# A hybrid decoder step on one core: no closing product per decode lot, two heads' state products side by side, and the elementwise work ahead of the recurrence in 32 pieces

## The chip, the cores and the metric

One core of a Trainium2 chip runs the whole step in one launch. The metric is the device time of that core in microseconds (us). Engines are named as in the profile: PE is TensorE (PEld its weight loads), DVE is VectorE, ACT is ScalarE, POOL is GpSimd, SP is SyncE, which here only issues DMAs.

## The reference

One layer of a hybrid trunk reads 512 prompt tokens (plus 16 learned meta tokens) and 8 running sequences of 8 new tokens each. All arrays are float32, the model width is 1024. Of the normalised input a combined projection makes the inputs of eight forgetting-attention heads and of eight RWKV-7 heads of width 64:

```python
logits = q.k / sqrt(64) + c_q[t] - c_k[s]        # c: running sum of log forget gates
out    = softmax(logits over past pages and own tokens) @ v

kk = k * k_k;  kk = kk / max(norm(kk), 1e-12)    # per head
k  = k * (1 + (a - 1) * k_a)
# per token, state S (64 x 64) of each head
S  = S * decay + (S @ -kk) (kk * a)^T + v k^T;   y = S @ r
out = (groupnorm(y) + sum(r * k * r_k) * v) * g
```

The decode sequences attend to 4096 past tokens each, that is 32 pages of 128 tokens out of a paged cache; keys and values of all pages, 134 MB, pass through the core once. Both head groups go through one output projection, a residual, a SwiGLU feed-forward part of width 2816 and a last norm. The updated RWKV states, the new keys and values and the shift rows are outputs too.

## The kernel before

The step runs in stages. First come the norms, the input projection and the prompt's attention (up to about 329 us in the profiled execution). Then follow, woven together, the decode attention over the cache and all of the RWKV work (329 to 912 us). Last come the output projection and the feed-forward part (912 us to the end), which the change doesn't touch.

**The decode lots.** The sequences are taken in four pairs, each pair's pages in eight lots of four pages: 32 lots. On each engine a lot is a generator of eight pieces. On PE these are: turn the keys of page pair 0 (`turn_keys`, L1178); keys of pair 1 and scores of pair 0 (`page_scores`, L1192); turn the probabilities of the lot before (`turn_probs`, L1218); keys 2 and scores 1; first half of the values of the lot before (`lot_values`, L1237); keys 3 and scores 2; second half of the values; scores 3. After the second half of a lot's values stands one small product, L1241: the identity times a column of ones, added into column 511 of the output bank, which `add_output` doesn't read; its end raises `ov_ready`. In the same pieces ACT copies the turned keys out of PSUM (L1622) and takes the exponentials (L1628), and DVE copies the probabilities (L2131, piece 2), adds a lot's output to the running one (`add_output`, L2141, piece 6) and adds bias to the scores and takes their maximum (`add_scores`, L2100 to L2107, piece 7).

**The rest of the work.** All RWKV work is a second generator per engine (`rwkv_rest`), cut into 140 pieces. After each lot piece every engine takes as many rest pieces as `rwkv_due` says: a straight line, one piece by lot piece 0 and all 140 by lot piece 236 of 256. All engines use the same table, and what they owe each other is kept by semaphores. Each engine works strictly in the order written.

**Ahead of the recurrence.** The first 17 rest pieces are `rwkv_pre`, the elementwise work on 128 x 2560 tiles (four head pairs of 640 token columns): keys scaled and squared, the row sums and their root and reciprocal (L1881, L1502, L1884), eight low-rank products (L868, taken by a sigmoid on ACT, L1495), the norms spread back and multiplied in (L854, L1868), a running sum of the log decays (L1888), three exponentials of 128 x 2560 on ACT (L1517 to L1521), products of all of these (L1893 to L1926, mostly one instruction of 2560 columns each) and the bonus sums (L886, L1872). A tile of the recurrence starts with L962.

**The DMA queue.** SP issues pages in the order in which lots use them, each once the slot it lands in is free. Ahead of a lot's keys stands the load of its forget biases. The bias rows of the second lot land where the low-rank weights lie, so their load, and all that is queued behind it (the keys of the third lot first), waits for the eighth low-rank product to be taken (`lr_taken` at 8).

**The sample states.** Near lot 24 the new states of the 8 running sequences are made, per pair of heads g: DVE spreads two operands per head (`Um`, L2043, two buffers), PE multiplies the keys (L1108) and then the `B` rows (L1109) of head 2g, then those of head 2g+1, each 64 rows by 64 columns by 512, and DVE adds and scales (L2031, L2035).

## Time and profile before

| what | value |
|---|---|
| median of 3 runs | 1510.46 us (1509.58 to 1511.0) |
| profiled execution | 1510.73 us, of which the span from first to last instruction is 1509.0 us |
| mean granted TensorE clock | 0.969 |
| PE busy | 1402.4 us, 93% of the span |
| DVE, ACT, POOL busy | 438.2 us, 357.0 us, 110.0 us |
| DMA | 219.32 MB, 145 GB/s over the span |

The busy share is a mean over stages with different limits. From 984 us to the end PE runs almost without a gap; the stretch in which the other engines and the DMA queues matter lies between 329 and 912 us, and that is where the changed lines are.

### The profile page before, as it was taken

To read this page: it belongs to the slowest core of one execution; us is meant where nothing else is said; L and a number is where in the kernel's file an instruction comes from. 1 tells how busy PE (TensorE), PEld (TensorE's weight loads), DVE (VectorE), ACT (ScalarE), POOL (GpSimd) and SP (SyncE) were. 2 spreads that over 40 slices of the span, in tenths; PEclk is the share of its full clock that TensorE was granted. 3 is DMA by queue.
4 is the path that set the end of the run, shared out by engine and by line. 5 is a ranking of instruction groups with operands and counts; after the bars stand their busy time and mean duration, and the time that the engine had idled before them with its cause. 6 is when DMAs were issued, how large, how long until landed. Compare 5 with 4: busy or idle time off the path is not lost.

```text
span 1509.0 us, 27895 instructions
## 1 busy us (share of the span) xinstructions
PE 1402.4 (93%) x11595; PEld 953.3 (63%) x11595; DVE 438.2 (29%) x917; ACT 357.0 (24%) x713; POOL 110.0 (7%) x223
## 2 busy tenths in 40 slices
PE   5999999988799999999989779999999999999997
PEld 4755666655577777777755454477777777744442
DVE  5022355455844444444445241310000000000002
ACT  3010233245444343443433331100000000000011
POOL 6283000000000000001202010000000000000000
PEclk9999899998799999999989889999999999999998
DMA  5187011023898787878957897003111221150001
GB/s 206 57 189 205 7 57 35 1 75 110 284 312 277 229 292 247 294 255 266 272 191 261 315 314 245 1 13 100 56 56 56 89 79 56 56 195 0 0 0 63
DMA packets 123174, 219.32 MB, mean 145 GB/s; under 512 B 11451, under 2 KB 35078, under 8 KB 123046
## 3 DMA queue, kind: packets, MB, share of 16 engines
q1 hardware_dynamic: 115154, 193.64, 38.3%
q0 software_dynamic: 7824, 23.85, 5.9%
q8 instruction: 92, 1.51, 0.4%
q14 instruction: 36, 0.29, 0.1%
q10 hardware_dynamic: 68, 0.02, 0.0%
HBM read 203.06 MB, written 14.41 MB: 144 GB/s over the span
## 4 chain that ended last, share of the span: by engine, by line
PE 84%; DVE 5%; DMA 4%; ACT 3%; issue 2%; SPq 1%; POOL 0%; DVEq 0%; POOLq 0%; ACTq 0%
PE PS L1369 23%; PE PS L736 13%; PE PS L1388 10%; PE PS L1178 6%; PE PS L1192 4%; PE PS L1308 4%; PE PS L1237 4%; PE PS L709 2%; DMA arena<-in_cache_k 2%; DMA out_wkv_prompt<-arena 1%; PE PS L1394 1%; PE PS L992 1%; PE PS L1002 1%; PE PS L996 1%; ACT arena L1622 1%
## 5 line engine op out<-in xcount | busy, mean ns | idle before, releaser
L1369 PE MATMUL PS<-arena 128*128 128x288 f32 x1408 | 342.1, 405 | 1.2 <-DVE arena L2251 1.2
L1369 PEld LDWEIGHTS PS<-arena 128*128 128x128 f32 x1408 | 265.7, 189 | 77.4 <-DVE arena L2251 1.4
L736 PE MATMUL PS<-arena 128*128 128x301 f32 (+1 forms) x736 | 197.7, 426 | 0.0
L1622 ACT ACTIVATE arena<-PS 128x512 f32<-128x512 f32 x256 | 141.4, 596 | 192.8 <-PE PS L1178 192.4
L1178 PE MATMUL PS<-arena 128*128 128x128 f32 x1024 | 153.8, 296 | 27.1 <-DMA arena<-in_cache_k 15.1
L736 PEld LDWEIGHTS PS<-arena 128*128 128x128 f32 (+1 forms) x736 | 136.6, 189 | 54.7 <-issue 13.6
L1178 PEld LDWEIGHTS PS<-arena 128*128 128x128 f32 x1024 | 122.1, 151 | 55.8 <-issue 24.2
L1388 PE MATMUL PS<-arena 128*128 128x512 f32 x352 | 151.5, 592 | 1.5 <-DVE arena L2277 1.5
L1388 PEld LDWEIGHTS PS<-arena 128*128 128x128 f32 x352 | 66.5, 189 | 86.2 <-issue 84.3
L2277 DVE TENSOR_TENSOR arena<-PS,arena 128x576 f32<-128x576 f32 x22 | 16.7, 758 | 327.0 <-ACT arena L1686 327.0
L1686 ACT ACTIVATE arena<-PS 128x576 f32<-128x576 f32 x22 | 14.3, 651 | 329.8 <-PE PS L1369 329.8
L1192 PE MATMUL PS<-arena 128*32 128x128 f32 x2048 | 85.7, 286 | 3.8 <-ACT arena L1622 2.4
L1237 PE MATMUL PS<-arena 128*32 128x256 f32 x1024 | 69.7, 389 | 2.8 <-DMA arena<-in_cache_v 2.8
L1192 PEld LDWEIGHTS PS<-arena 128*32 128x32 f32 x2048 | 50.0, 112 | 24.8 <-issue 19.3
L1308 PE MATMUL PS<-arena 128*128 128x512 f32 x128 | 55.8, 593 | 0.0
L1952 DVE TENSOR_TENSOR arena<-PS,arena 128x512 f32<-128x512 f32 (+2 forms) x56 | 35.9, 659 | 41.3 <-PE PS L992 20.6
L2297 DVE TENSOR_TENSOR arena<-PS,arena 128x512 f32<-128x512 f32 x8 | 5.5, 692 | 143.2 <-PE PS L1388 143.2
L363 POOL DMA_DIRECT2D out_y_prompt<-arena x4 | 2.1, 537 | 596.0 <-DVE arena L2286 596.0
L1671 ACT ACTIVATE arena<-arena 128x1024 f32<-128x1024 f32 x8 | 8.4, 1045 | 151.4 <-DVE arena L2297 137.7
L1237 PEld LDWEIGHTS PS<-arena 128*32 128x32 f32 x1024 | 29.5, 111 | 22.3 <-issue 6.4
L1308 PEld LDWEIGHTS PS<-arena 128*128 128x128 f32 x128 | 23.9, 189 | 29.1 <-issue 29.1
L1434 ACT ACTIVATE arena<-PS 128x602 f32<-128x602 f32 (+1 forms) x23 | 15.5, 673 | 108.3 <-PE PS L736 108.3
(360 smaller groups left out, 1409.9 us busy)
## 6 DMA issues: line engine op xcount, KB each, us to landing
arena<-in_cache_k SPq DMA_DIRECT2D x256, 256.0 KB, 4.3
arena<-in_cache_v SPq DMA_DIRECT2D x256, 256.0 KB, 4.8
arena<-in_w_gate SPq DMA_DIRECT2D x11, 1024.0 KB
arena<-in_w_up SPq DMA_DIRECT2D x11, 1024.0 KB
arena<-in_w_in SPq DMA_DIRECT2D x5, 2048.0 KB, 11.9
forgets_after<-arena POOLq DMA_DIRECT2D x64, 128.0 KB, 8.5
arena<-forgets_after SPq DMA_DIRECT2D x32, 256.0 KB, 5.1
arena<-in_w_down SPq DMA_DIRECT2D x4, 2048.0 KB
```

Of the source, the lines that this page charges most:

```text
L709: ins = mm(o, xnT[:, k, 17 + P * (i - 1):17 + P * i], w, start=(k == 0), stop=(k == KT - 1))
L736: ins = mm(PS[0:width, bank, 0:HALF], wring[:, c % 2, k, c0:c0 + width], xnT[:, k, half * HALF:(half + 1) * HALF], start=(k == 0), stop=(k ...
L1178: ins = tr(PS[:, bank, g * P:(g + 1) * P], Kr[:, i, q, g * P:(g + 1) * P], ident)
L1192: ins = mm(PS[ROWS[2 * q + gp], SCORE, i * P:(i + 1) * P], QB[:, 2 * (L // NLOT) + q, g, :], KTs[:, (2 * i + q) % LOT, g, :], start=(gg == ...
L1237: ins = mm(PS[ROWS[r], OUT, 0:QW], PTs[:, i, ROWS[r]], Vr[:, i, r // 2, QW * (r % 2):QW * (r % 2) + QW], start=(i == 0), stop=(i == LOT - ...
L1308: ins = mm(PS[rows, E + 2 * (n % 2) + half, :], mixT[:, k, cols], wo[:, k, half * NB:(half + 1) * NB], start=(k == 0), stop=(k == KT - 1))
L1369: ins = mm(PS[:, 4 * (f % 2) + 2 * w + half, 0:HO], fring[r % FR][:, c:c + P], hT[:, k, half * HO:(half + 1) * HO], start=(k == 0), stop=( ...
L1388: ins = mm(PS[:, 4 * half + n, :], actT[:, k, cols], w_down(half, k), start=(k == 0), stop=(k == NF - 1))
L1434: av(dst.rearrange("p (a b) -> p a b", a=2), src, ACT.Copy, scale=scale).then_inc(S["proj_taken"], 1)
L1622: av(KTs[:, (2 * i + q) % LOT], PS[:, T_USE[("k", L, i, q)] % 2, :].rearrange("p (g n) -> p g n", g=NG), ACT.Copy)\
L1952: return tt(dst, src, mask.unsqueeze(1).unsqueeze(1).to_broadcast([n_p, a, b, n]), ALU.mult)
L2277: tt(actT[:, f, :].rearrange("p (a b) -> p a b", a=2), PS[:, 4 * (f % 2) + 2:4 * (f % 2) + 4, 0:HO], sgate[:, f % 2, :].rearrange("p (a b) ...
```

## The change

Three edits. (1) The product L1241 is gone; `add_output` now waits for `v_free`, the semaphore that the last value product of the lot raises anyway. (2) The sample state products of head 2g and 2g+1 are issued alternately, keys of both, then `B` rows of both, after one wait for both heads' operands. (3) `rwkv_pre` has 32 pieces in place of 17. Its operations of 2560 columns are cut into two of 1280 (the reciprocal into two of 320), the running sums stand one to a piece, and empty pieces on PE and ACT keep step with DVE. `rwkv_due` gives two rest pieces to lot piece 0 and one to each of the next 30; the other 123 pieces follow on a straight line, complete by lot piece 235. The order of SP's and POOL's instructions is the same as before.

```diff
-        N_PRE = 17
+        N_PRE = 32
...
         def rwkv_due(piece):
-            return min(N_RWKV, 1 + piece * (N_RWKV - 1) // (8 * LOTS - 20))
+            if piece < N_PRE - 1:
+                return piece + 2
+            left, pieces = N_RWKV - N_PRE - 1, 8 * LOTS - 20 - N_PRE
+            return min(N_RWKV, N_PRE + 1 + (piece - N_PRE + 1) * left // pieces)
...
-                if half:
-                    mm(PS[:, OUT, 511:512], ident, ones[:, 0:1], start=False, stop=True, skip_group_check=True).then_inc(S["ov_ready"], 1)
...
             def add_output(L):
                 q = L // NLOT % 2
-                dve.wait_ge(S["ov_ready"], L + L // NLOT + 2)
+                dve.wait_ge(S["v_free"], LOT * (L + 2))
...
                 for g in range(NG):
-                    for hp in range(2):
-                        h = 2 * g + hp
-                        hc = slice(h * HD, (h + 1) * HD)
-                        pe.wait_ge(S["um_ready"], h + 1)
...
+                    pe.wait_ge(S["um_ready"], 2 * g + 2)
+                    if g >= 2:
+                        pe.wait_ge(S["sn_taken"], g - 1)
+                    for w, u in ((K_, 1), (B_, 0)):
+                        for hp in range(2):
+                            hc = slice((2 * g + hp) * HD, (2 * g + hp + 1) * HD)
+                            ins = mm(PS[64 * hp:64 * hp + 64, E + 2 + g % 2, :], nat_[64:P, w, hc],
+                                     Um[64:P, hp, u].rearrange("p b i -> p (b i)"), start=(u == 1), stop=(u == 0), skip_group_check=True)
...
-                v.reciprocal(Rn, Rn).then_inc(S["hs_in"], 1)
+                ch(v.reciprocal(Rn[:, 0:HT], Rn[:, 0:HT]))
+                yield
+                v.reciprocal(Rn[:, HT:TL], Rn[:, HT:TL]).then_inc(S["hs_in"], 1)
+                yield
+                norm_keys(0)
+                yield
+                for g in range(3):
+                    dve.wait_ge(S["lr_taken"], g + 1)
+                    ch(v.tensor_tensor_scan(Kd[:, g], chunk_mask, AR[:, 0, g], 0.0, ALU.mult, ALU.add))
+                    norm_keys(g + 1)
+                    yield
...
-                ch(tt(Bd, Bd, kk, ALU.mult))
+                for p in pair:
+                    ch(tt(Bd[:, p], Bd[:, p], kk[:, p], ALU.mult))
+                    yield
```

On PE, around the second lot: keys (L1178, after the change L1186), scores (L1192, then L1200), probabilities (L1218, then L1226), values (L1237, then L1245), low-rank products (L868, then L871) and spread norms (L854, then L857). Before:

```order
L1218 MATMUL PS<-arena 128x128 x4
L1178 MATMUL PS<-arena 128x128 x8
L1192 MATMUL PS<-arena 32x128 x8
L868 MATMUL PS<-arena 128x320 x2
L854 MATMUL PS<-arena 128x320 x2
L1237 MATMUL PS<-arena 32x256 x8
L868 MATMUL PS<-arena 128x320 x2
L1178 MATMUL PS<-arena 128x128 x8
L1192 MATMUL PS<-arena 32x128 x8
L1237 MATMUL PS<-arena 32x256 x8
L1241 MATMUL PS<-arena 128x1
L1192 MATMUL PS<-arena 32x128 x8
```

The same place after the change, from the lot's second key pages on:

```order
L1186 MATMUL PS<-arena 128x128 x8
L1200 MATMUL PS<-arena 32x128 x8
L871 MATMUL PS<-arena 128x320 x2
L1226 MATMUL PS<-arena 128x128 x4
L1186 MATMUL PS<-arena 128x128 x8
L1200 MATMUL PS<-arena 32x128 x8
L1245 MATMUL PS<-arena 32x256 x8
L1186 MATMUL PS<-arena 128x128 x8
L1200 MATMUL PS<-arena 32x128 x8
L1245 MATMUL PS<-arena 32x256 x8
L1200 MATMUL PS<-arena 32x128 x8
```

The last low-rank product stood behind the first half of the values, in lot piece 12; it now stands ahead of the lot's probabilities, in lot piece 9. The closing product ahead of the last scores is gone.

On DVE, the pieces behind the low-rank products, in lots 1 and 2: L1902 and L1905 to L1915 are elementwise work, L2141 is `add_output`, L2100 to L2107 `add_scores`, L2125 and L2127 the running sums, L2131 the copy of the probabilities. Before:

```order
L1902 TENSOR_SCALAR arena<-arena 128x640 x4
L2141 SCALAR_TENSOR_TENSOR arena<-arena,PS 128x256
L1905 SCALAR_TENSOR_TENSOR arena<-arena 128x2560
L2100 TENSOR_TENSOR arena<-PS,arena 128x512
L2103 TENSOR_REDUCE arena<-arena 128x1
L2107 TENSOR_SCALAR arena<-arena 128x1
L1909 SCALAR_TENSOR_TENSOR arena<-arena 128x640 x4
L2125 SCALAR_TENSOR_TENSOR arena<-arena 128x1
L2127 TENSOR_TENSOR arena<-arena 128x1
L1913 TENSOR_TENSOR arena<-arena 128x2560
L2131 COPY arena<-PS 128x512
L1915 SCALAR_TENSOR_TENSOR arena<-arena 128x2560
```

After the change the same lines are L1916, L2169, L1921, L2128 to L2135, L1926, L2153 and L2155, L2159 and L1934:

```order
L1916 TENSOR_SCALAR arena<-arena 128x640 x4
L2169 SCALAR_TENSOR_TENSOR arena<-arena,PS 128x256
L1921 SCALAR_TENSOR_TENSOR arena<-arena 128x1280
L2128 TENSOR_TENSOR arena<-PS,arena 128x512
L2131 TENSOR_REDUCE arena<-arena 128x1
L2135 TENSOR_SCALAR arena<-arena 128x1
L1921 SCALAR_TENSOR_TENSOR arena<-arena 128x1280
L1926 SCALAR_TENSOR_TENSOR arena<-arena 128x640 x2
L2153 SCALAR_TENSOR_TENSOR arena<-arena 128x1
L2155 TENSOR_TENSOR arena<-arena 128x1
L1926 SCALAR_TENSOR_TENSOR arena<-arena 128x640 x2
L2159 COPY arena<-PS 128x512
```

Between two operations of a lot there now stand one or two halves where one or two whole operations stood.

On PE, the sample state products of the third pair of heads (L1108 and L1109 before, L1115 after). Before:

```order
L1178 MATMUL PS<-arena 128x128 x16
L1192 MATMUL PS<-arena 32x128 x8
L1108 MATMUL PS<-arena 64x512
L1109 MATMUL PS<-arena 64x512
L1108 MATMUL PS<-arena 64x512
L1109 MATMUL PS<-arena 64x512
L1218 MATMUL PS<-arena 128x128 x4
```

After the change:

```order
L1186 MATMUL PS<-arena 128x128 x8
L1115 MATMUL PS<-arena 64x512 x4
L1186 MATMUL PS<-arena 128x128 x8
L1200 MATMUL PS<-arena 32x128 x8
L1226 MATMUL PS<-arena 128x128 x4
```

This group of four moved one lot piece up, ahead of the second key pages; the first two groups keep their lot piece.

## Rows read from the trace of the kernel before

**Rows 1.** Stretch, us; busy PE, PEld, DVE, ACT, POOL; PE clock, DMA share, GB/s.

```profile
335.61:415.62 80.01, 65.74 (x555) 43.42 (x555) 53.69 (x58) 41.03 (x56) 1.75 (x5) 0.80 0.60 206
421.00:774.00 353.00, 332.66 (x6383) 260.28 (x6381) 148.48 (x321) 149.38 (x295) 13.36 (x17) 1.00 0.82 269
```

**Rows 2.** PE's waits in 802 to 912 us: total, times, longest.

```profile
PE PS L1178 <- DMA arena<-in_cache_k: 7.9, 3, 5.3
PE PS L1237 <- DMA arena<-in_cache_v: 2.8, 3, 1.3
```

**Rows 3.** The closing product by line: busy, mean ns, idle before.

```profile
L1241 PE MATMUL PS<-arena 128*128 128x1 f32 x64 | 12.3, 261 | 0.0
```

**Rows 4.** PE in time, end of lot 2: start, us, count.

```profile
395.26 1.09 PE L1178 MATMUL PS<-arena 128*128 128x128 f32 x8
396.28 0.65 PE L1192 MATMUL PS<-arena 128*32 128x128 f32 x16
396.75 1.05 PE L1237 MATMUL PS<-arena 128*32 128x256 f32 x16
397.72 0.38 PE L1241 MATMUL PS<-arena 128*128 128x1 f32 x2
398.04 0.65 PE L1192 MATMUL PS<-arena 128*32 128x128 f32 x16
398.61 1.09 PE L1178 MATMUL PS<-arena 128*128 128x128 f32 x8
```

**Rows 5.** Busy time by stretch: lots 0, 1, 2 and 3 up to L962.

```profile
335.61:360.27 24.66, 21.16 (x150) 12.80 (x151) 15.82 (x13) 12.68 (x17) 0.00 (x0) 0.78 0.64 220
360.27:382.28 22.01, 17.54 (x155) 11.36 (x154) 12.49 (x15) 15.60 (x18) 0.00 (x0) 0.89 0.21 66
382.28:398.61 16.33, 13.81 (x134) 9.73 (x134) 13.31 (x16) 7.73 (x12) 0.00 (x0) 0.61 1.01 359
398.61:415.62 17.01, 13.23 (x121) 9.53 (x117) 12.07 (x16) 5.03 (x10) 1.75 (x5) 0.90 0.63 220
```

**Rows 6.** PE in time, waits in brackets, elementwise stretch.

```profile
350.99 1.34 PE L854 MATMUL PS<-arena 32*128 32x320 f32 x4 [0.67 <-DVE arena L1884]
...
357.88 2.46 PE L854 MATMUL PS<-arena 32*128 32x320 f32 x4 [2.64 <-DVE arena L1868]
...
382.28 3.83 PE L1178 MATMUL PS<-arena 128*128 128x128 f32 x16 [3.98 <-DMA arena<-in_cache_k]
...
407.68 3.57 PE L886 MATMUL PS<-arena 128*128 128x320 f32 x8 [3.78 <-DVE arena L1872]
```

**Rows 7.** ACT and SP in time: last low-rank sigmoid, bias load.

```profile
374.98 0.80 ACT L1495 ACTIVATE arena<-PS,arena 128x640 f32<-128x640 f32 x1 [2.76 <-PE PS L868]
...
375.80 0.82 SPq L428 DMA_DIRECT2D arena<-forgets_after  x2
```

**Rows 8.** DVE by line and shape, 335.61 to 415.62 us.

```profile
L1888 DVE TENSOR_TENSOR_SCAN arena<-arena 128x640 f32<-128x640 f32 x4 | 5.6, 1472 | 0.3 <-ACT arena L1495 0.3
L1909 DVE SCALAR_TENSOR_TENSOR arena<-arena 128x640 f32<-128x640 f32 x4 | 3.3, 878 | 0.0
L1905 DVE SCALAR_TENSOR_TENSOR arena<-arena 128x2560 f32<-128x2560 f32 x1 | 2.8, 2818 | 0.0
```

**Rows 9.** Sample states in time, second and third pair of heads.

```profile
782.40 2.32 PE L1108 MATMUL PS<-arena 64*64 64x512 f32 x3 [2.79 <-DVE arena L2043]
...
787.21 3.83 PE L1178 MATMUL PS<-arena 128*128 128x128 f32 x16
...
790.93 2.50 DVE L2043 TENSOR_TENSOR arena<-arena 64x512 f32<-64x512 f32 x4
...
792.28 1.07 PE L1108 MATMUL PS<-arena 64*64 64x512 f32 x2 [0.65 <-DVE arena L2043]
...
793.49 0.64 PE L1108 MATMUL PS<-arena 64*64 64x512 f32 x1
...
795.35 0.66 PE L1218 MATMUL PS<-arena 128*128 128x128 f32 x4
```

More of the change, by code:

```diff
@@ L889, in rwkv_pre @@
             def rwkv_pre():
-                yield
+                for _ in range(3):
+                    yield
                 row_sums_of(T2, 1, E + 2)
@@ L905, in rwkv_pre @@
                 yield
-                for _ in range(6):
+                for _ in range(8):
                     yield
@@ L910, in rwkv_pre @@
                 yield
+                for _ in range(9):
+                    yield
                 bonus_sums(2)
                 bonus_sums(3)
+                yield
                 yield
@@ L1497, in rwkv_pre @@
             def rwkv_pre():
-                yield
+                for _ in range(3):
+                    yield
                 low_rank(0)
@@ L1505, in rwkv_pre @@
                 yield
-                low_rank(3)
                 yield
-                low_rank(4)
+                for j in range(3, 8):
+                    low_rank(j)
+                    yield
                 yield
-                low_rank(5)
-                yield
-                low_rank(6)
-                yield
-                low_rank(7)
                 yield
@@ L1522, in rwkv_pre @@
                 yield
-                for _ in range(7):
+                for _ in range(16):
                     yield
@@ L1900, in rwkv_pre @@
                 dve.wait_ge(S["lr_taken"], 8)
-                for g in range(NG):
-                    ch(ts(T2[:, g], Bd[:, g], -1.0, pc("k_a", g), ALU.add, ALU.mult))
-                yield
-                ch.wait()
-                ch(stt(XR[:, 4:8], T2, 1.0, XR[:, 4:8], ALU.add, ALU.mult))
-                yield
-                ch.wait()
-                for g in range(NG):
-                    ins = stt(T2[:, g], XR[:, g], pc("r_k", g), XR[:, 4 + g], ALU.mult, ALU.mult)
-                ins.then_inc(S["hs_in"], 1)
@@ L1921, in rwkv_pre @@
-                ch(tt(Bd, Bd, Kd, ALU.mult))
-                yield
-                ch(tt(AR[:, 1], XR[:, 0:4], AR[:, 1], ALU.mult))
-                yield
-                ch.wait()
-                ch(tt(Kd, XR[:, 4:8], Kd, ALU.mult))
-                yield
+                for p in pair:
+                    for g in range(p.start, p.stop):
+                        ch(ts(T2[:, g], Bd[:, g], -1.0, pc("k_a", g), ALU.add, ALU.mult))
+                    yield
+                for p in pair:
+                    ch.wait()
+                    w = slice(4 + p.start, 4 + p.stop)
+                    ch(stt(XR[:, w], T2[:, p], 1.0, XR[:, w], ALU.add, ALU.mult))
+                    yield
@@ new lines, in rwkv_pre @@
+                for p in pair:
+                    ch.wait()
+                    for g in range(p.start, p.stop):
+                        ins = stt(T2[:, g], XR[:, g], pc("r_k", g), XR[:, 4 + g], ALU.mult, ALU.mult)
+                        if g < 3:
+                            ch(ins)
+                    if p.stop == NG:
+                        ins.then_inc(S["hs_in"], 1)
+                    yield
+                dve.wait_ge(S["decays"], 3)
+                for p in pair:
+                    ch(tt(Bd[:, p], Bd[:, p], kk[:, p], ALU.mult))
+                    yield
@@ new lines, in rwkv_pre @@
+                for p in pair:
+                    ch(stt(AR[:, 0, p], kk[:, p], -1.0, AR[:, 0, p], ALU.mult, ALU.mult))
+                    if p.start == 0:
+                        ch(v.tensor_copy(Dc[:, :, 0:1], AR[:, 1, :, NMETA - 1:NMETA]))
+                        ch(v.tensor_copy(Dc[:, :, 1:1 + DB], AR[:, 1, :, 64 + DS - 1:P:DS]))
+                        ch(v.tensor_copy(Dc[:, :, 1 + DB:], AR[:, 1, :, P + 63:TL:64]))
+                    yield
+                for p in pair:
+                    ch.wait()
+                    ch(tt(Bd[:, p], Bd[:, p], Kd[:, p], ALU.mult))
+                    yield
@@ L1928, in rwkv_pre @@
+                for p in pair:
+                    ch.wait()
+                    ch(tt(AR[:, 1, p], XR[:, p], AR[:, 1, p], ALU.mult))
+                    yield
+                for p in pair:
+                    ch.wait()
+                    ch(tt(Kd[:, p], XR[:, 4 + p.start:4 + p.stop], Kd[:, p], ALU.mult))
+                    yield
                 add_bonus(0)
@@ L1932, in rwkv_pre @@
                 add_bonus(3)
+                yield
                 ch.wait()
```

41 lines of the change are left out of this document (17 added, 24 removed).

## Prediction, made before the changed kernel was timed

> **What bounds the kernel now.** I read busy time by stretch first, since a share over the whole span mixes stages. Two stretches differ. In 421 to 774 us, most of the woven decode and recurrence part, PE is busy 332.66 of 353 us at full clock [rows 1]: PE is the bound, and an instruction taken off PE there comes off the time. In 335.61 to 415.62 us, the lots that share the engines with the elementwise work, PE is busy 65.74 of 80.01 us and its granted clock is only 0.80 [rows 1]: PE waits, and pays twice, since it comes back from long waits at the lower of its two clock levels, 1.2 GHz (a spread product takes 2.46 us behind a wait of 2.64 us and 1.34 us behind one of 0.67 us [rows 6]). So I then read who is waited for there: a running sum on DVE (2.64 us), keys by DMA (3.98 us) and the bonus products on DVE (3.78 us) [rows 6]. Last, from 802 to 912 us, PE's waits for page DMAs alone come to 10.7 us [rows 2]: what PE saves ahead of such a wait is waited for instead.
>
> **The closing product.** L1241 has 64 records, two per product, so 32 products of 0.38 us busy each, with no idle time before them [rows 3]. What one is worth is the step from its start to the next instruction's: 398.04 - 397.72 = 0.32 us [rows 4]. `add_output` loses nothing: its new semaphore is raised by the product just before. Of the 32, two lie in the elementwise stretch and are counted there. Four (those in lots 26, 27, 29 and 30) stand ahead of the waits for DMA after 802 us, which end at their own time [rows 2]; I give them nothing. The other 26 give 26 x 0.32 = 8.3 us. Between none hidden (30 x 0.32 = 9.6) and all given back as waits (0) I take 8.3, because PE has hardly any idle time in the stretch where 20 of them lie.
>
> One more effect could be in this edit. Scores take 0.47 us when values of the same 128 x 32 shape follow (396.28 to 396.75), but 0.57 us when a 128 x 128 product follows (398.04 to 398.61) [rows 4]. The Trainium skill, TensorEngine Tiling (Array Packing), Key Properties, says why that may be: changing the tiling mode drains the engine. By that rule the sixteen lots in which scores followed directly on L1241 would gain about 0.1 us more each, 1.6 us in all, and the sum would be 1493.7 us. The two rows agree with it, but none shows values followed by scores, so I leave it out of the sum.
>
> **The elementwise stretch.** It runs through lots 0 to 3. I walk through it on the rows' durations at full clock: keys of one page pair 1.02 us, scores 0.57, values 0.97 [rows 4], probabilities half of the keys, 0.51, a low-rank or spread product about 1.3 [rows 6]. A lot's own PE work without the closing product is then 4 x 1.02 + 4 x 0.57 + 2 x 0.97 + 0.51 = 8.8 us. On DVE the four running sums take 5.6 us and stand in one piece; an operation on 2560 columns takes 2.8 us [rows 8]. Cutting costs something: four instructions of 640 columns are busy 3.3 us where one of 2560 takes 2.8, so 0.15 us more for each extra instruction; nine cuts, 1.4 us.
>
> Lot 0, 24.66 us before [rows 5]. Up to the first spread at 350.99 us nothing moves, because row sums, root and reciprocal are one chain that PE already waits for [rows 6]. Behind it PE waited 2.64 us for all four running sums and came back at half clock. Now one sum of 1.4 us stands ahead of each norm, and PE has its low-rank and spread products to do meanwhile: from 352.3 us, 4 x 1.3 us, scores 0.6 and the new tokens' values 0.6 end at 358.8. So 23.2 us, with two more low-rank products done.
>
> Lot 1, 22.01 us before. Its end was the wait of 3.98 us for keys. They came late because SP's bias load waits for the eighth low-rank sigmoid, which ended at 375.78, and went out at 375.80 [rows 7]; meanwhile the DMA engines were busy 0.21 of the time, and in the next lot 1.01 [rows 5]. The eighth product moves from lot piece 12 to piece 9; by my walk its sigmoid ends near 368 us, the keys can be in use 6.5 us later, as they were before (375.80 to 382.28) [rows 6, 7], so near 374, when PE comes to them. PE's own work is 8.8 + three products of 1.3 = 12.7 us; ACT, with three exponentials on 2560 columns, is the later one, and was busy 15.6 us in this lot before [rows 5]. The walk gives 15.3 us.
>
> Lot 2, 16.33 us before. DVE sets it: it was busy 13.31 us [rows 5] and is given one half more (1.5 us) and four cuts, 15.4 us, and PE waits for the last exponential on ACT. The walk gives 16.1 us: no gain here beyond the closing product.
>
> Lot 3, 17.01 us before up to the first recurrence tile. That tile now comes two lot pieces later, behind values (1.0) and scores (0.6), so 18.6 us is what to compare with. DVE has four halves, the bonus products and the memsets behind each other; the walk gives 18.9 us. The wait of 3.78 us goes, but the second pair of bonus sums, now in the piece just ahead of DVE's second pair of additions, waits for DVE's queue instead.
>
> Together 23.2 + 15.3 + 16.1 + 18.9 = 73.5 us against 80.0 + 1.6 = 81.6: a gain of 8.1 us. The walk is at full clock; waits of 1 to 3 us stay, after which some products run at 1.2 GHz; I take 1 us off for that and enter 7.1 us. Bounds: nothing (81.6), and DVE never waiting in lots 1 to 3, where it was busy 12.49 + 13.31 + 12.07 us and gets 1.4 on top: 39.3 us, with lot 0 62.5, a gain of 19.1. Behind the stretch the recurrence starts two pieces later and ends one piece earlier, at nearly the same density; I enter nothing.
>
> **The sample states.** DVE makes the operands of a pair of heads in 2.50 us; PE starts the first head when its half is there (792.28) and the second at 793.49, and the next work follows at 795.35 [rows 9]. So the second head's own passes take 1.86 us, and the first head's run beside them already. With both heads started at 793.49 the group ends at 795.35 too: zero. The bounds are a loss of 1.21 us per group if the alternating products get in each other's way (4.8 us for four), and a gain if DVE were ahead.
>
> The Trainium skill would have that gain: TensorEngine Tiling (Array Packing), Key Properties, says that different tiles execute independently, weight loads and products in parallel. The trace agrees that they overlap, and for that reason already in the old order; the page names no wait for operands.
>
> **Sum.** 8.3 + 7.1 + 0 = 15.4 us. The profiled execution took 1510.73 us (span 1509.0 and 1.7 around it), 0.27 above the median of the runs; 1510.7 - 15.4 = 1495.3 us. The likeliest case's own range is 1489 to 1501.
>
> **Rivals.**
> - Only the closing products count (1501.7). DVE has the same work plus 1.4 us, so its queue moves PE's waits from one piece to the next and the stretch stays as long; 28 x 0.32 = 9.0 us come off (all but the four). For it: DVE was busy 53.69 of 80.01 us [rows 1] and sets lots 2 and 3 in my walk. Against: the 3.98 us for keys hang on one early release, not on DVE. Chance 0.17.
> - The stretch gives all that DVE allows: 19.1 + 8.3 off, 1483.3 us. For it: pieces of 1.5 us fit into PE's 8.8 us per lot everywhere. Against: ACT's three long exponentials are not cut. Chance 0.11.
> - The sample operands are ready early, and side by side pays: each group then costs 1.86 us and not 3.07 (792.28 to 795.35), the group at 1.2 GHz twice 1.86 and not 4.81 [rows 9]; 3 x 1.21 + 1.09 = 4.7 us more, 1490.6 us. Against: PE waits for DVE at both starts in the rows. Chance 0.07. This is the way it would go by the Trainium skill's rule on independent tiles.
> - No change (1510): a lot's period is the loop scores, maximum, exponential, probabilities, and what PE saves comes back as waits in it, in the stretch too. Against: PE idles 20 us in 353 [rows 1]. Chance 0.05.
> - Slower: in lots 1 to 3 DVE now always holds a half, so PE gets many short waits, and its clock stays at 1.2 GHz through them. PE's work there in my walk, some 35 us, takes 70 us where the walk has 50.3: 20 us more, 1515 us. It decides from the point where three quarters of those lots run at 1.2 GHz. For it: lot 2 had a clock of 0.61 before [rows 5]. Against: that low clock stood behind the wait for keys. Chance 0.05.
>
> **How the numbers follow.** The forecast has 0.55. What a measurement of this kernel can tell from no change is about 0.2%, 3 us, so faster means below 1507.4: the forecast and the first three rivals, 0.90, less 0.02 for their tails. Same gets 0.05 + 0.02, slower 0.05. The range leaves out half of the second rival and both last ones: 1484 to 1507 us.
>
> **What would show it.** The chain and the lines must have no L1241, and the step from values to scores must be gone. In the stretch up to the first L970 (the old L962), the bias load behind the last low-rank sigmoid must go out some 8 us earlier, and the first key product of lot 2 must not wait for DMA; the stretch itself should be near 73.5 us long with a clock above 0.80. In the sample states, PE should wait about 1.2 us longer at each start and end each group as before. 421 to 774 us should shrink by about 0.32 us per lot and PE's idle time there stay near 20 us. I am wrong if that idle time grows by what the closing products were worth, or if DVE's work shows PE's waits in lots 2 and 3 to be longer than the ones that went.

## The result and the profile after

The changed kernel took 1523.54 us, median of 4 runs (1518.33 to 1530.8), against 1510.47 (1509.58 to 1511.0) for the kernel before: a ratio of 1.009, 95% interval 1.0046 to 1.0135. It is slower by 7 to 20 us, where 15 us faster was forecast, and its single runs lie 12 us apart. On a second chip the two stood at 1520.91 and 1510.04 us, a ratio of 1.0059 (1.0034 to 1.0084). One execution of 2046.56 us, among the twelve of the kernel with an early bias load and the recurrence two pieces ahead further down, lies far outside the rest and is left out of that kernel's ratio.

The profiled execution took 1518.33 us (span 1516.5). Its mean granted clock of TensorE was 0.957, where the kernel before had 0.969.

To compare stretches I cut them at two events that both kernels have: PE's first row-sum product, and the addition of lot 3's scores on DVE. Of before, and then of after (columns as in [rows 1]):

```profile
340.24:419.69 79.45, 65.19 (x588) 42.48 (x580) 53.73 (x61) 39.76 (x54) 1.75 (x5) 0.83 0.59 201
```

```profile
339.25:420.25 81.00, 70.06 (x558) 43.67 (x549) 52.80 (x66) 38.97 (x52) 0.14 (x1) 0.75 0.60 205
355.00:360.00 5.00, 5.00 (x30) 1.96 (x28) 3.75 (x6) 0.00 (x0) 0.00 (x0) 0.50 0.08 31
360.00:365.00 5.00, 5.00 (x14) 3.10 (x14) 2.50 (x3) 1.66 (x3) 0.00 (x0) 0.50 0.00 0
365.00:370.00 5.00, 5.00 (x11) 2.47 (x11) 0.47 (x2) 3.14 (x5) 0.00 (x0) 0.50 0.00 0
370.00:375.00 5.00, 5.00 (x28) 2.99 (x27) 2.05 (x4) 2.64 (x5) 0.00 (x0) 0.50 0.02 3
375.00:380.00 5.00, 5.00 (x44) 3.49 (x44) 3.99 (x5) 3.42 (x5) 0.00 (x0) 0.50 0.53 161
```

PE's idle time in the stretch fell from 14.3 to 10.9 us, as intended, and PE had 30 records less. Yet its busy time grew by 4.9 us. From 355 to 380 us PE is busy in every microsecond and has 1.2 GHz throughout. PE in order of time, after (start, us, form, count):

```profile
352.07 1.43 PE L871 MATMUL PS<-arena 64*128 64x320 f32 x4
353.44 2.49 PE L857 MATMUL PS<-arena 32*128 32x320 f32 x4
355.86 1.08 PE L1200 MATMUL PS<-arena 128*32 128x128 f32 x16
356.87 1.08 PE L1234 MATMUL PS<-arena 64*32 64x256 f32 x8
357.88 2.50 PE L871 MATMUL PS<-arena 64*128 64x320 f32 x4
360.31 2.50 PE L857 MATMUL PS<-arena 32*128 32x320 f32 x4
362.73 1.97 PE L1186 MATMUL PS<-arena 128*128 128x128 f32 x8
```

L871 are the low-rank products (64 rows of the array), L857 the spread products (32 rows). A spread product took 1.34 us at full clock [rows 6], and a low-rank product as much; here either takes 2.5. No wait stands between them, and the last one before them ended at 348.36 us: the clock fell at about 353 us in the middle of work. The last low-rank sigmoid therefore ended as late as before [rows 7], and the bias load went out at 375.75 us, not 8 us earlier:

```profile
374.93 0.79 ACT L1501 ACTIVATE arena<-PS,arena 128x640 f32<-128x640 f32 x1 [1.54 <-PE PS L871]
...
375.75 0.81 SPq L431 DMA_DIRECT2D arena<-forgets_after  x2
```

The prediction measured the stretch from the first key product of lot 0 to the first recurrence tile, and had it near 73.5 us. Here it takes 85.57 us:

```profile
334.62 3.84 PE L1186 MATMUL PS<-arena 128*128 128x128 f32 x16 [2.67 <-DMA arena<-in_cache_k]
...
420.19 1.09 PE L970 MATMUL PS<-arena 64*64 64x128 f32 x16 [1.33 <-DVE arena L1964]
```

The first key products of lots 1, 2 and 3 start at 362.73, 383.73 and 400.54 us. So lots 0 to 3 take 28.1, 21.0, 16.8 and 19.7 us, where the walk had 23.2, 15.3, 16.1 and 18.9: nearly all of the excess lies in lots 0 and 1, where the clock was low.

In 421 to 774 us PE's idle time is 21.7 us, near the 20.3 of before [rows 1]:

```profile
421.00:774.00 353.00, 331.33 (x6376) 259.06 (x6374) 150.59 (x324) 151.14 (x297) 14.19 (x21) 1.00 0.81 269
```

The four groups of the sample states now wait 1.30, 3.99, 0.69 and 3.32 us for DVE, where only two of them waited before (2.79 and 0.65 us), and three of the four then run wholly or partly at 1.2 GHz (3.68, 3.67 and 3.20 us for a group, 1.94 at full clock). The first two, to be compared with [rows 9]:

```profile
773.47 1.94 PE L1115 MATMUL PS<-arena 64*64 64x512 f32 x8 [1.30 <-DVE arena L2071]
...
782.59 3.68 PE L1115 MATMUL PS<-arena 64*64 64x512 f32 x8 [3.99 <-DVE arena L2071]
```

### The profile page after: what moved, and what is told of

It is laid out like the page before. It is cut to its first block, busy times and chain, and to the rows that moved or that the text cites. A ratio compares the mean times of both kernels' runs of the same rounds, so it can differ in the third digit from the quotient of the medians.

```text
span 1516.5 us, 27778 instructions
## 1 busy us (share of the span) xinstructions
PE 1405.3 (93%) x11531; PEld 951.7 (63%) x11531; DVE 438.7 (29%) x926; ACT 358.4 (24%) x713; POOL 110.1 (7%) x223
## 4 chain that ended last, share of the span: by engine, by line
PE 85%; DVE 5%; ACT 3%; DMA 3%; issue 2%; SPq 1%; POOL 0%; DVEq 0%; POOLq 0%; ACTq 0%
PE PS L1375 23%; PE PS L739 12%; PE PS L1394 10%; PE PS L1186 7%; PE PS L1200 4%; PE PS L1314 4%; PE PS L1245 4%; PE PS L712 2%; PE PS L1400 1%; DMA arena<-in_cache_k 1%; DMA arena<-in_cache_v 1%; PE PS L1010 1%; PE PS L1000 1%; PE PS L1004 1%; ACT arena L1626 1%
## 5 line engine op out<-in xcount | busy, mean ns | idle before, releaser
L1186 PE MATMUL PS<-arena 128*128 128x128 f32 x1024 | 154.2, 295 | 35.7 <-DVE arena L2159 13.5
L739 PEld LDWEIGHTS PS<-arena 128*128 128x128 f32 (+1 forms) x736 | 135.7, 188 | 54.2 <-issue 12.7
L1186 PEld LDWEIGHTS PS<-arena 128*128 128x128 f32 x1024 | 121.6, 150 | 67.0 <-issue 32.6
L1690 ACT ACTIVATE arena<-PS 128x576 f32<-128x576 f32 x22 | 14.3, 652 | 332.7 <-PE PS L1375 332.7
L1200 PE MATMUL PS<-arena 128*32 128x128 f32 x2048 | 87.9, 291 | 1.6 <-DVE arena L2146 0.8
L1245 PE MATMUL PS<-arena 128*32 128x256 f32 x1024 | 72.1, 399 | 4.4 <-DMA arena<-in_cache_v 4.4
L1200 PEld LDWEIGHTS PS<-arena 128*32 128x32 f32 x2048 | 52.8, 114 | 26.9 <-issue 19.6
L1245 PEld LDWEIGHTS PS<-arena 128*32 128x32 f32 x1024 | 30.0, 113 | 24.6 <-issue 7.7
```

The costliest lines, as they stand in the source:

```text
L739: ins = mm(PS[0:width, bank, 0:HALF], wring[:, c % 2, k, c0:c0 + width], xnT[:, k, half * HALF:(half + 1) * HALF], start=(k == 0), stop=(k ...
L1186: ins = tr(PS[:, bank, g * P:(g + 1) * P], Kr[:, i, q, g * P:(g + 1) * P], ident)
L1200: ins = mm(PS[ROWS[2 * q + gp], SCORE, i * P:(i + 1) * P], QB[:, 2 * (L // NLOT) + q, g, :], KTs[:, (2 * i + q) % LOT, g, :], start=(gg == ...
L1245: ins = mm(PS[ROWS[r], OUT, 0:QW], PTs[:, i, ROWS[r]], Vr[:, i, r // 2, QW * (r % 2):QW * (r % 2) + QW], start=(i == 0), stop=(i == LOT - ...
```

## Experiments

Ratios are to the kernel before, run on the same chip, with 95% intervals; differences in us are the ratio less one, times the median of before there (1510 to 1512 us).

### Each edit by itself

**The first edit alone.** The kernel before with the two lines of the closing product taken out and DVE's two waits set to match:

```diff
-                if half:
-                    mm(PS[:, OUT, 511:512], ident, ones[:, 0:1], ...).then_inc(S["ov_ready"], 1)
...
-                dve.wait_ge(S["ov_ready"], L + L // NLOT + 2)
+                dve.wait_ge(S["v_free"], LOT * (L + 2))
...
-                dve.wait_ge(S["ov_ready"], (NLOT + 1) * pr + 1)
+                dve.wait_ge(S["ov_ready"], pr + 1)
```

> The kernel before with the first edit alone: the 32 closing products are gone. Theory A (each closing product was worth its step of 0.32 us wherever PE has no idle time): 8 to 9 us come off, 1501 to 1503 us, and PE's idle time in the woven part stays near 20 us. Rival B (PE is not the bound of a lot: what it saves comes back as waits): 1509 to 1512 us. Rival C (the loss of the whole change lies in this edit, because the full-array product helped to hold the clock up): 1515 us or more, with a lower granted clock in lots 4 to 23.

Measured: 1505.54 us, 0.9957 (0.9935 to 0.9979), so 6.5 us less (3.2 to 9.8): theory A in its mechanism, its 8 to 9 us at the upper end. Lots 4 to 8 by the windows of before and of this kernel (both from one addition of scores on DVE to another):

```profile
419.69:498.88 79.19, 74.99 (x1422) 58.27 (x1425) 34.39 (x72) 34.01 (x69) 0.00 (x0) 1.00 0.85 287
```

```profile
419.52:497.04 77.52, 73.31 (x1412) 56.87 (x1414) 34.34 (x73) 33.99 (x69) 0.00 (x0) 1.00 0.87 295
```

Five lots, five closing products, 1.67 us: 0.33 us each. Its granted clock there is 1.00, as it is on to lot 23, so rival C falls. In these two profiles the gain is larger than the run's: from the first row-sum product to the scores of lot 31 the kernel before takes 571.91 us and this one 563.91, 8.0 us less; behind that point, where both do the same work, this one takes 2.8 us more (599.68 against 596.85), most of it at the first gate and up products (last section).

**The second edit alone.**

```diff
-                    for hp in range(2):
...
-                        pe.wait_ge(S["um_ready"], h + 1)
...
+                    pe.wait_ge(S["um_ready"], 2 * g + 2)
...
+                    for w, u in ((K_, 1), (B_, 0)):
+                        for hp in range(2):
...
```

> The kernel before with the second edit alone: each pair of sample heads waits for both operands and runs side by side. Theory A (the trace of the changed kernel shows four waits on DVE there, a granted clock of 0.50 from 780 to 806 us, and lot 25 6.0 us longer): 3 to 6 us slower, 1513.5 to 1516.5 us. Rival B (the group ends when it did, as predicted; what is longer in lot 25 came from rest work left over from earlier): 1509.5 to 1511.5 us. Rival C (side by side pays): below 1508 us.

Measured: 1513.72 us, 1.0003 (0.9982 to 1.0024): 0.5 us more, between 2.7 less and 3.6 more. That is nothing that can be measured. It fits rival B, and theory A is out but for its lower end.

**The third edit alone.** The changed kernel with the closing products and the old order of the sample heads put back.

> The kernel before with the third edit alone: the elementwise work in 32 pieces, closing products and the old order of the sample states kept. Theory A (the loss lies in the elementwise stretch: PE stays at 1.2 GHz for about 27 us there, though it is busy): 8 to 15 us slower, 1518 to 1525 us, with granted clock 0.50 from about 355 to 380 us and single runs some us apart. Rival B (the stretch gains its 7 us and the loss is elsewhere): 1503 to 1506 us. Rival C (the closing product between values and scores holds the clock up in the stretch, so that with it the pieces do no harm): 1508 to 1511 us and a clock above 0.75 from 355 to 380 us.

Measured: 1525.28 us, 1.0081 (1.0051 to 1.0112): 12.3 us more (7.7 to 16.9). Theory A; the clock is 0.50 in each 5 us from 355 to 380 us, with PE busy 5.00 of 5, closing products or not. The loss lies in this edit.

**The first two edits without the third.**

> The changed kernel without its third edit: no closing products and the sample heads side by side, elementwise work in 17 pieces as before. Theory A (the three edits add up: closings -8, heads +3 to +6): 1505 to 1508 us. Rival B (all of the loss is the pieces): 1501 to 1503 us. Rival C (the pieces do no harm): 1520 us or more, as the changed kernel.

Measured: 1510.17 us, 0.9986 (0.9962 to 1.0009): 2.1 us less, between 5.7 less and 1.4 more: rivals B and C are out, and theory A's sum fits, though the loss that it gives the heads did not show in the run of the second edit alone. The three edits by themselves add up to -6.5 + 0.5 + 12.3 = +6.3 us; all of them together are 8.9 (5.1 to 12.7) on the second chip.

### Why PE is slow in the pieces

**Full rows.** Same products, same columns, same result, but over all 128 rows, with weights that GpSimd pads with zeros beforehand:

```diff
+            ch(g.memset(WZ, 0.0))
+            ch(g.memset(SZ, 0.0))
+            for r in range(2):
+                ch(g.tensor_copy(WZ[64 * r:64 * r + 64, r], WA[64 * r:64 * r + 64]))
+            for q in range(NG):
+                ch(g.tensor_copy(SZ[32 * q:32 * q + 32, q], spread[32 * q:32 * q + 32]))
...
-                    ins = mm(..., spread[rows], Rn[rows, ...
+                    ins = mm(..., SZ[:, g], Rn[:, ...
...
+                if j == 0:
+                    pe.wait_ge(S["pool_c"], WIDE[0])
...
-                    ins = mm(..., WA[rows, w], XR[rows, 12, ...
+                    ins = mm(..., WZ[:, j // 4, w], XR[:, 12, ...
```

> The changed kernel, but its 8 low-rank and 4 spread products of the elementwise stretch contract over all 128 rows instead of 64 and 32: GpSimd copies their weights into blocks padded with zeros beforehand, so each product has the same columns, the same result and the same number of passes. Theory A (PE stays at 1.2 GHz there because most of its work uses few of the array's rows): granted clock above 0.85 from 355 to 380 us, these products near 1.3 us and not 2.5, and the kernel 8 to 14 us below the changed one, 1509 to 1516 us. Rival B (the clock follows the many small pieces and waits, whatever the rows): clock 0.50 as before, 1522 to 1525 us.

Measured: 1508.87 us, 0.9983 (0.9965 to 1.0002); the changed kernel beside it had 1520.91. 12.0 us less by the medians, by no other edit than the rows and the padding ahead of them (the new wait for GpSimd's copies shows no idle time on PE). The windows, and PE in order of time (L883 low-rank, L868 spread):

```profile
343.73:412.47 68.74, 55.10 (x558) 36.77 (x549) 52.58 (x67) 38.15 (x52) 0.07 (x1) 0.91 0.71 241
355.00:360.00 5.00, 5.00 (x36) 2.95 (x38) 3.40 (x4) 1.59 (x2) 0.00 (x0) 1.00 0.79 285
360.00:365.00 5.00, 5.00 (x30) 3.51 (x23) 4.93 (x8) 2.06 (x4) 0.00 (x0) 1.00 0.09 33
```

```profile
354.57 1.35 PE L883 MATMUL PS<-arena 128*128 128x320 f32 x4
355.75 1.24 PE L868 MATMUL PS<-arena 128*128 128x320 f32 x4
```

The stretch takes 68.74 us, with 558 records; in the two profiles of the changed kernel it takes 81.00 us (558 records) and 77.89 us (559, the one on the same chip). Theory A holds, and rival B is out.

**Filler.** The narrow products as they are, and a product of 128 rows ahead of each but the first:

```diff
+            def fill(bank):
+                mm(PS[:, bank, 0:256], ident, XR[:, 8, 0:256], start=True, stop=True, ...)
```

> The changed kernel with 11 more products in the elementwise stretch, of 128 rows, 128 columns of weights and 256 columns, one ahead of each low-rank (but the first) and each spread product, into the bank that this product then overwrites: at full clock about 0.5 us each, 5.6 us of work that nothing needs. Theory A (rows of the array hold the clock): the clock from 355 to 380 us rises above 0.75 and the kernel comes out no slower than the changed one, 1513 to 1523 us, in spite of the added work. Rival B (the rows don't matter): clock 0.50, the fillers take 1 us each, 8 to 12 us slower than the changed kernel.

Measured: 1514.63 us, 1.0028 (1.0006 to 1.005): 6.3 us below the changed kernel by the medians, though PE has 11 products more (L861 here). The intervals of the two ratios overlap, so the size of that gain is uncertain; the clock is not, it is 1.00 in each 5 us from 355 to 380 us:

```profile
342.84:416.46 73.62, 61.62 (x582) 38.76 (x574) 52.88 (x66) 39.01 (x53) 0.14 (x1) 0.95 0.68 229
360.00:365.00 5.00, 5.00 (x38) 2.51 (x37) 3.99 (x6) 0.79 (x1) 0.00 (x0) 1.00 0.01 2
```

```profile
361.73 0.70 PE L861 MATMUL PS<-arena 128*128 128x256 f32 x2
362.36 1.34 PE L876 MATMUL PS<-arena 64*128 64x320 f32 x4
...
364.26 1.34 PE L857 MATMUL PS<-arena 32*128 32x320 f32 x4
```

So narrow products run at full clock when full-row work stands between them: it is the long run of them that PE does at 1.2 GHz, not the single product.

**The old order with full rows.** The first edit and full rows in the order of before.

> The kernel before without its closing products (the first edit alone) and with the low-rank and spread products over all 128 rows. Theory A: in the order of before these products ran at full clock but for one behind the wait of 2.64 us, so little is to be had: 0 to 3 us below the first edit alone, 1499 to 1505 us. Rival B (a wait brings the clock down and the rows of what follows don't matter): the same as the first edit alone, 1502 to 1507 us.

Measured: 1502.21 us, 0.9933 (0.9908 to 0.9959). The intervals of this and of the first edit alone (0.9957) overlap; the times fit either expectation.

**The changed kernel again**, beside these three.

> The changed kernel as it is, on the same chip as the three others, so that they can be set against it and not only against the kernel before. By all theories 1518 to 1526 us, 8 to 16 us above the kernel before, with granted clock 0.50 from about 355 to 380 us.

Measured: 1520.91 us, 1.0059 (1.0034 to 1.0084), with a clock of 0.50 from 355 to 370 us.

### Where the forecast gain of the stretch is

**An early bias load in the old order.** The padded copies make the original low-rank weights, which lie where the second bias lands, free early:

```diff
                 elif j == 1:
-                    sp.wait_ge(S["lr_taken"], 8)
+                    sp.wait_ge(S["pool_c"], 97)
```

> The kernel before without closing products, low-rank and spread products over 128 rows, and SyncE's second bias load waits only for GpSimd's copies of the low-rank weights (it lands where the original weights lie), not for the eighth sigmoid. The 17 pieces and their order stay. If the 3.98 us that PE waited for keys hang on this one release, as the prediction has it, the wait of 4.5 us ahead of lot 2's keys goes without any cutting of the elementwise work: 2 to 5 us below the same kernel with the late release, 1497 to 1501 us where that had 1502. Rival (the wait is only passed on, to ACT's exponentials, as the changed kernel shows 3.36 us behind them): no change, 1501 to 1504 us, with a wait of 3 us or more on ACT in its place.

Measured: 1502.07 us, 0.9931 (0.9907 to 0.9956), the same as without it. The load went out at 354.85 us, and PE waited nonetheless. The wait ahead of lot 2's keys, first with the late load and then with the early one:

```profile
379.24 3.38 PE L1190 MATMUL PS<-arena 128*128 128x128 f32 x16 [4.49 <-DMA arena<-in_cache_k]
```

```profile
385.41 1.94 PE L1190 MATMUL PS<-arena 128*128 128x128 f32 x8 [4.53 <-ACT arena L1632]
```

This is the rival's case: L1632 is ACT's copy of turned keys, which stands behind the long exponentials. In the changed kernel the same wait has 3.36 us.

**Pieces, full rows, old order of the heads** (the changed kernel with full rows less its second edit).

> The first and the third edit with the low-rank and spread products over 128 rows, sample heads in the old order: the changed kernel with full rows less its second edit. If the second edit costs 2 to 4 us in this setting: 1505 to 1507 us. If it costs nothing: 1508 to 1510 us, as with it.

Measured: 1507.37 us, 0.9973 (0.9956 to 0.9989): the expectation for a second edit that costs something, but the interval overlaps that of the run with it (0.9983). Its windows show what the stretch is worth: to lot 3, to lot 12, lots 13 to 17, and lots 18 to 31. First the old order with full rows, then the pieces:

```profile
339.18:417.44 78.26, 61.47 (x584) 41.52 (x576) 53.62 (x62) 39.84 (x54) 1.74 (x5) 0.87 0.58 203
339.18:562.03 222.85, 197.61 (x3331) 147.81 (x3322) 116.30 (x193) 102.81 (x179) 1.74 (x5) 0.95 0.75 256
562.03:649.50 87.47, 83.16 (x1600) 66.05 (x1604) 39.10 (x88) 34.43 (x69) 0.00 (x0) 0.98 0.76 257
649.50:901.68 252.18, 216.90 (x3113) 154.28 (x3112) 103.51 (x204) 100.30 (x185) 24.78 (x35) 0.94 0.81 275
```

```profile
339.49:410.02 70.53, 57.22 (x560) 38.71 (x549) 52.66 (x66) 38.38 (x52) 0.07 (x1) 0.88 0.69 235
339.49:553.10 213.61, 193.21 (x3243) 144.90 (x3232) 117.01 (x202) 100.94 (x176) 1.74 (x5) 0.96 0.78 264
553.10:648.42 95.32, 87.58 (x1694) 68.72 (x1691) 39.05 (x88) 36.29 (x71) 0.00 (x0) 0.96 0.75 246
648.42:906.16 257.74, 221.95 (x3112) 155.26 (x3111) 103.53 (x204) 100.54 (x185) 24.74 (x35) 0.91 0.80 268
```

Each kernel has one profile here, and they are from two chips. The pieces lead by 7.7 us at lot 3 and 9.2 at lot 12, but PE has then done 88 records less (3243 against 3331). In lots 13 to 17 it does them (1694 against 1600), with 7.7 us of idle time against 4.3, 2.9 of them one wait of a recurrence step for DVE. At lot 17, with 4937 records against 4931, the lead is 310.32 - 308.93 = 1.4 us; against the old order with the early bias load, which gets there in 306.25 us with 4936 records, it is a lag of 2.7 us. Behind it the same work takes 5.6 us longer, nearly all of it clock (0.91 against 0.94; idle 35.8 and 35.3). Most of that last part varies between profiles, and the old order with the early bias load took 257.75 us for it too. One piece of it is steady: lots 24 to 26 take 73.50 us at a clock of 0.84 here, and 71.93 us at 0.91 in the old order. In the five profiles with neither the pieces nor the heads side by side these lots take 71.85 to 72.40 us at 0.90 to 0.93; in the eight with one or both (and the recurrence not moved ahead) 73.50 to 76.19 us at 0.80 to 0.88. Why the clock is lower there, these runs don't show.

With full rows the clock can fall too. In this run it was 0.50 from 350 to 353 us, after a wait of 1.66 us that ended at 348.44 us; it was back at 1.00 by 354 us while PE worked on. With the narrow rows it stayed at 0.50 for 25 us.

**The recurrence two pieces ahead**, with the early bias load.

```diff
+            ahead = 0 if piece < N_PRE + 8 else 1 if piece < N_PRE + 16 else 2
-            return min(N_RWKV, N_PRE + 1 + (piece - N_PRE + 1) * left // pieces)
+            return min(N_RWKV, N_PRE + 1 + ahead + (piece - N_PRE + 1) * left // pieces)
```

> As the run with the recurrence two pieces ahead, and with the early bias load as well. In the 32 pieces the keys of lot 2 no longer waited for DMA, but PE waited for ACT there; so the early load gives nothing more: within 2 us of the run without it. If it does give something, 2 to 4 us less.

Measured: 1515.98 us, 1.0029 (1.0012 to 1.0046); with the table alone 1514.94, 1.0028 (1.001 to 1.0047).

> The first and third edit with full rows, sample heads in the old order (1507 us, 0.9973 of before), and from lot piece 40 on the recurrence one and from 48 on two pieces ahead of the changed kernel's table, so that it is no longer behind the old one. Theory (the late recurrence costs a wait of 2.9 us where a pair of lots changes, and what was put off is paid for in lots 12 to 17): 2 to 5 us off, 1502 to 1505 us. Rival (put-off work costs the same wherever it is done): 1506 to 1509 us. With the early bias load as well it took 1516 us: if that lies in the table, 1513 to 1518 us here.

A table that is two pieces ahead from the end of the 32 pieces on deadlocks (engines wait for each other in a circle), so it has no time.

So the load costs and gives nothing, and the table costs 8 us (0.9973 without it). The theory's gain is not there: the wait of 2.9 us stays (waits of PE: us in total, times, longest), and the table brings a new wait of PE behind the recurrence. ACT, which works in the order written, now comes early to the square of 128 x 2560 that has to wait until the prompt's new states are written out (12.12 us, 6.94 us without the table), and the copies of turned keys that PE needs in lot 27 stand behind it (L1199 are key turns):

```profile
PE PS L1023 <- DVE arena L1993: 3.1, 2, 2.9
```

```profile
831.76 2.34 ACT L1621 ACTIVATE arena<-arena 128x2560 f32<-128x2560 f32 x1 [12.12 <-DMA out_wkv_prompt<-arena]
```

```profile
835.32 1.94 PE L1199 MATMUL PS<-arena 128*128 128x128 f32 x8 [10.91 <-ACT arena L1639]
```

**Filled waits in the old order.** Products that nothing needs, put into three of PE's long waits, on top of the first edit and full rows:

```diff
+                if (L, i) == (2, 0):
+                    pe.wait_ge(S["ov_taken"], 2)
+                    fill(OUT, XR[:, 8, 0:256], 7)
                 pe.wait_ge(k_in[i], 32 * (L + 1))
...
+                pe.wait_ge(S["ov_taken"], 3)
+                fill(OUT, XR[:, 8, 0:256], 6)
                 bonus_sums(2)
...
+            fill(E + 3, mixT[:, 0, 0:256], 2)
             turn_h(4)
+            fill(E + 3, mixT[:, 0, 0:256], 2)
```

> The order of before without closing products and with 128-row low-rank and spread products (1502 us, 0.9933 of before), and with products that nothing needs put into PE's own long waits: 7 ahead of the keys of lot 2, 6 ahead of the third bonus product, 2 and 2 around the last turn ahead of gate and up, each of 128 rows, 128 columns of weights and 256 columns (about 0.5 us). Theory (PE comes back from a long wait at 1.2 GHz, and filling the wait keeps it at full clock for free): granted clock from 380 to 390 us above 0.9 (0.66 and 0.68 without), the third and fourth bonus products 2.3 us and not 4.6, clock 1.00 at the first gate and up products, and 2 to 6 us off: 1496 to 1500 us. Rival (what runs at 1.2 GHz there lies beside DVE's and ACT's work, which sets the end): the rows get faster but the time stays within 1501 to 1503 us.

Measured: 1498.13 us (1494.2 to 1504.96), 0.9925 (0.9894 to 0.9955). The third and fourth bonus products without and with it:

```profile
404.52 4.61 PE L898 MATMUL PS<-arena 128*128 128x320 f32 x8 [3.78 <-DVE arena L1882]
```

```profile
401.32 2.76 PE L1189 MATMUL PS<-arena 128*128 128x256 f32 x12
405.28 2.40 PE L898 MATMUL PS<-arena 128*128 128x320 f32 x8 [1.20 <-DVE arena L1893]
```

The rows do what was expected there, and the clock at the first gate and up products is 1.00; but from 385 to 390 us it is 0.77, behind waits for ACT that I had not filled. The median is in the expected range; against 0.9933 without the fillers the gain isn't shown. It has the lowest median here, some 11 us below the kernel before on the same chip (7 to 16).

## Why the prediction was wrong

**The step that failed** is the one of the elementwise stretch: "The walk is at full clock; waits of 1 to 3 us stay, after which some products run at 1.2 GHz; I take 1 us off for that". I knew one way to the low clock, a wait, and priced that. The change took PE's waits away and put the twelve narrow products close together, and PE fell to 1.2 GHz in the middle of them and stayed there.

The sign stood in the trace of the kernel before, and I read it wrongly. I put the spread product of 2.46 us [rows 6] down to the wait of 2.64 us ahead of it. But the low-rank product ahead of that wait already took 1.82 us, so the clock had fallen before the wait began; in the old order with full rows the same product in the same place took 1.35 us. First before, then with full rows:

```profile
353.41 1.82 PE L868 MATMUL PS<-arena 64*128 64x320 f32 x4
```

```profile
352.23 1.35 PE L880 MATMUL PS<-arena 128*128 128x320 f32 x4
```

A wait brings the clock down as well: behind it (3.11 us there) the spread product took 2.47 us with full rows too, at a granted clock of 0.50. By line, busy in the stretch, after (32 and 16 records each):

```profile
L871 PE MATMUL PS<-arena 64*128 64x320 f32 x32 | 14.0, 576 | 0.0
L857 PE MATMUL PS<-arena 32*128 32x320 f32 x16 | 8.8, 695 | 0.0
```

and with full rows:

```profile
L883 PE MATMUL PS<-arena 128*128 128x320 f32 x32 | 10.4, 451 | 0.0
...
L868 PE MATMUL PS<-arena 128*128 128x320 f32 x16 | 5.0, 434 | 0.0
```

That is 22.8 against 15.4 us, 7.4 of the 12.3 us by which the stretches of these two profiles differ; keys, scores and values between them, and what waits for them, make the rest.

**The walk itself** was right, once the narrow products no longer hold the clock down. With full rows lots 0 to 3 take 23.6, 14.4, 15.9 and 19.4 us, 73.3 in all (75.1 in the run with the old order of the heads), where the walk had 73.5. In the latter run the bias load goes out at 367.56 us, where I had it near 368. This is shown by changing the rows alone.

**A second step failed with it**: "Behind the stretch the recurrence starts two pieces later and ends one piece earlier, at nearly the same density; I enter nothing". The late start had to be entered as work put off. At equal work, in lot 17, the pieces with full rows are 1.4 us ahead of one profile of the old order and 2.7 us behind the other. So even with full rows this term was worth about nothing there and not 7.1 us, and the whole kernel is slower for the pieces (below). By the medians the narrow rows account for 12.0 of the miss of some 24 us on the second chip (15.4 us less forecast, 8.9 us more measured), and the pieces with full rows for about as much (7.1 us forecast as a gain, 5.3 us measured as a loss).

**The keys' wait.** I argued that the 3.98 us "hang on one early release, not on DVE". The release was not enough: ACT's copies behind its exponentials end 4.5 us late as well, and the early load showed it. I had ACT as the later engine in lot 1 of the walk, and "ACT's three long exponentials" against a rival, but left ACT out of this argument.

**The closing products** were sized right: 8.3 us forecast, 6.5 (3.2 to 9.8) measured, and 8.0 up to lot 31 in the profiles. What I had not seen is the 2.8 us behind that point. The side effect that I left out of the sum is there. The step from values to the following scores is 0.86 us in this kernel of the first edit (903.42 - 902.56), where values took 0.97 [rows 4]:

```profile
902.56 1.05 PE L1237 MATMUL PS<-arena 128*32 128x256 f32 x16
903.42 0.62 PE L1192 MATMUL PS<-arena 128*32 128x128 f32 x16
```

The Trainium skill, TensorEngine Tiling (Array Packing), Key Properties, has it that a change of tiling mode drains the engine; values and scores here have the same tile shape, and the row agrees, by 0.1 us. In the time it can't be seen.

**The sample states** came out as forecast, at nothing (0.5 us, -2.7 to 3.6), and the waits grew by 1.2 us as said (2.79 to 3.99). What I had not said is that PE then runs the group at 1.2 GHz more often; in the profile of the second edit alone lots 24 to 26 take 73.64 us and before 72.40, but the timing can't tell 1 us from nothing.

**The slower rival** (1515 us, chance 0.05) had the right place and sign: PE at 1.2 GHz through most of lot 1. Its reason, many short waits, was wrong, since PE had none from 353 to 380 us, and so it got too small a chance.

**What stays open.** With full rows the pieces are at 0.9973 (0.9956 to 0.9989), and the old order with the same products at 0.9933 (0.9908 to 0.9959). On the chip of the pieces the old order with the early load is at 0.9931 (0.9907 to 0.9956). So the forecast gain of 7 us is not there even with full rows: by the medians on that chip the pieces are 5.3 us slower, and the intervals meet only at their ends. The profiles put the difference behind lot 17, into the clock. Some 1.6 us of it, in lots 24 to 26, is steady; the rest varies between profiles of one kernel by more than that (258.94 and 266.81 us behind lot 17 in the two of the changed kernel), so where it arises stays open.

## What to carry to other kernels

Before packing small products closer together, look at how many rows of the array each uses: here a run of 64- and 32-row products cost PE half its clock though it never idled, and zero-padded weights of full rows, or full-row products in between, gave it back. A low clock behind a wait need not come from the wait: look at the last product ahead of it first. A lead inside a woven stretch counts only at equal work, so compare two orders at a point where both have done the same number of instructions. Where a wait ends with one engine, find out who would end it next before giving it a price.

## What the runs showed of the hardware

- PE was busy 5.00 of 5 us in five successive stretches and had 1.2 GHz in all of them; twelve products over 128 rows instead of 64 and 32 brought 2.4 GHz, and so did 11 useless full-row products between the narrow ones, with which the kernel was 6.3 us faster by the medians (the intervals overlap).
- Ahead of the first gate and up products PE does the same instructions with the same two waits (1.41 and 1.20 us) in every kernel but the one that fills them. Its clock in the 10 us around them was 1.00 in the profiles of the three kernels with closing products, and 0.66 or 0.83 in nine of the eleven profiles without them and without fillers there. After the change ACT had the first of their results 18.8 us after the first of these products (988.88 to 1007.68), before it 15.8 us (984.25 to 1000.09). I did not find the cause; with four full-row products in the two waits the clock was 1.00.
- The kernel before ranges from 1504.69 to 1521.49 us over 28 executions on one chip, with mean granted clocks from 0.959 to 0.973. Below some 3 us only the ratios of many runs tell anything here.
